# Last stage: rows of two tables fetched by one gather of 8 KB rows, or by two of 4 KB rows with rings of their own

## What is computed

```python
def _peer(h, wq, keys, u, v):              # h: tokens x 1024; u, v: 16384 x 1024
    q = (xt @ wq).reshape(P_BLOCK, P_HEADS, 2, P_HALF)
    s = jnp.einsum('nhpd,hpkd->nhpk', q, keys)
    ...
    top_s, pos = lax.top_k(cand_s, P_TOPK) # 16 picks for each of 8 heads
    idx = jnp.take_along_axis(cand_i, pos, axis=-1).reshape(P_BLOCK, P_HEADS * P_TOPK)
    g = jax.nn.softmax(...)
    act = jax.nn.gelu(jnp.einsum('nd,ned->ne', xt, u[idx]), approximate=False)
    return jnp.einsum('ne,ned->nd', g * act, v[idx])
```

## Time and profile before

| | us |
|---|---|
| median of 3 runs | 4033.4 |
| lowest, highest | 4031.19, 4033.41 |
| the profiled execution, its own time | 4033.23 |
| span of the profile, first to last instruction | 4031.5 |
| last stage: first gather issued to last gather issued | 2664.6 to 3996.7 |

### The profile page before, as it was taken

The page is one execution under the profiler, slowest core; times in us unless marked ns, Lnnn a source line. Parts: engine busy times, 40 slices in busy tenths (PEclk is TensorE's granted clock), DMA queues, the critical chain, the costliest instruction groups (busy, mean ns, idle before and its releaser), DMA issues. The chain is left out here.

```text
span 4031.5 us, 37513 instructions
## 1 busy us (share of the span) xinstructions
PE 3402.5 (84%) x11902; PEld 1525.5 (38%) x11903; DVE 1934.3 (48%) x3945; ACT 677.6 (17%) x1600; POOL 928.9 (23%) x811
## 2 busy tenths in 40 slices
PE   7988999668899978999868967689878888788877
PEld 3345444422333322333325445444333333333332
DVE  5834222522223323233325235476666766676676
ACT  1011211000000000000002125312222222222221
POOL 2000000021222222021221031014444444444443
PEclk9999999789999998999989988899999899999988
DMA  9825423369998999297975100239999999999997
GB/s 328 284 108 177 167 101 133 125 242 386 375 386 343 387 386 367 71 386 278 383 305 195 53 7 1 76 133 409 422 421 413 421 404 414 421 405 421 412 421 317
DMA packets 194149, 1157.36 MB, mean 287 GB/s; under 512 B 25659, under 2 KB 27995, under 8 KB 74356
## 3 DMA queue, kind: packets, MB, share of 16 engines
q1 hardware_dynamic: 97140, 565.17, 36.1%
q0 software_dynamic: 80576, 564.05, 34.2%
q10 hardware_dynamic: 16320, 26.75, 2.2%
HBM read 1128.96 MB, written 48.68 MB: 292 GB/s over the span
## 5 line engine op out<-in xcount | busy, mean ns | idle before, releaser
L2558 DVE SCALAR_TENSOR_TENSOR mod<-q_uv,mix 128x1024 f32<-128x1024 f32 x512 | 627.4, 1225 | 389.9 <-DMA q_uv<-in_peer_uv,q_picks 384.6
L1149 PE MATMUL ps<-wt,e_xT 128*64 128x512 f32 x3200 | 733.4, 613 | 94.4 <-DMA wt<-in_w_exp 93.6
L2263 POOL DMA_INDIRECT q_uv<-in_peer_uv,q_picks x512 | 571.2, 1116 | 996.6 <-PE ps L2355 719.1
L2355 PE MATMUL ps<-q_uv,q_dg 128*128 128x512 f32 x1024 | 491.6, 634 | 118.5 <-ACT q_dg L2432 118.3
L2355 PE MATMUL ps<-q_uv,tri 128*128 128x512 f32 x1024 | 494.3, 639 | 104.6 <-ACT tri L2432 104.6
L1129 POOL COPY wt<-e_land 128x2048 f32<-128x2048 f32 x124 | 237.1, 1912 | 1020.8 <-DMA e_land<-in_w_exp 1020.8
L1149 PEld LDWEIGHTS ps<-wt,e_xT 128*64 128x64 f32 x3200 | 238.3, 141 | 579.8 <-issue 433.2
L1149 PE MATMUL ps<-wt,e_aT 128*64 128x512 f32 x1600 | 357.4, 599 | 21.6 <-ACT e_aT L1202 21.6
L2355 PEld LDWEIGHTS ps<-q_uv,q_dg 128*128 128x128 f32 x1024 | 202.7, 203 | 398.6 <-issue 398.6
L2355 PEld LDWEIGHTS ps<-q_uv,tri 128*128 128x128 f32 x1024 | 205.6, 205 | 390.2 <-issue 390.2
L454 PE MATMUL ps<-hT,wt 128*128 128x512 f32 x640 | 285.0, 601 | 1.5 <-DVE wt L781 1.5
(11 more groups left out here) (446 smaller groups left out, 3329.8 us busy)
## 6 DMA issues: line engine op xcount, KB each, us to landing
wt<-in_w_exp SPq DMA_DIRECT2D x260, 1024.0 KB, 17.5
e_land<-in_w_exp SPq DMA_DIRECT2D x124, 1024.0 KB, 24.6
wt<-in_w_in_units SPq DMA_DIRECT2D x15, 2048.0 KB, 10.4
mod<-in_w_mod_units SPq DMA_DIRECT2D x48, 512.0 KB, 5.6
scratch_xs<-const_zeros SPq DMA_DIRECT2D x8, 2080.0 KB
mod<-in_w_ada_units SPq DMA_DIRECT2D x32, 512.0 KB, 6.5
p_ring<-in_w_in SPq DMA_DIRECT2D x7, 2048.0 KB, 10.4
e_xg<-scratch_xs ACTq DMA_DIRECT2D x104, 128.0 KB
```

The source lines that it names most:

```text
L1149: ins = nc.tensor.matmul(ps[64 * h:64 * h + 64, at, :], lhs[:, k % 4, 64 * (k // 4):64 * (k // 4) + 64], wt[:, u, a, h * W:(h + 1) * W], s ...
L2263: pool.indirect_dma_start(out=uv[:, n % NR, :, :].rearrange("p a d -> p (a d)"), out_offset=None, in_=A["peer_uv"], in_offset=bass.Indirec ...
L2355: last = nc.tensor.matmul(acc(t)[:, c, :], dg(n), uv[:, n % NR, 1, c * W:(c + 1) * W], start=fresh, stop=closing)
L2558: dve.scalar_tensor_tensor(junk[:, n % 2, :], uv[:, n % NR, 0, :], 1.0, mix[:, tile_of(k), :], ALU.mult, ALU.mult, accum_out=ap[:, k % 2, ...
```

## The change

Each step now fetches the row of `u` and the row of `v` by a transfer each, from two tables, 128 rows of 4 KB (512 KB) each. The memory of the ring is the same, now seen as 20 halves (`rows`): `NU` = 8 of them are a ring for `u`, given back by VectorE's dot (`s_u`), and `NV` = 12 are a ring for `v`, given back by TensorE (`s_v`). VectorE waits for the transfer of `u` alone, TensorE for that of `v` alone. GpSimd issues `u` of step `n`, then `v` of step `n`. The two waits at the start of the stage are moved to the first `v` slots that lie on the keys and the projection.

```diff
         uv = sb("uv", [P, NR, 2, D])
+        NU, NV = 8, 2 * NR - 8
+        rows = uv[:, :, :, :].rearrange("p n a d -> p (n a) d")
...
-        s_uv = [sem(f"uv{i}") for i in range(NR)]
+        s_gu = [sem(f"gu{i}") for i in range(NU)]
+        s_gv = [sem(f"gv{i}") for i in range(NV)]
...
                 for n in range(TOTAL):
                     if n % BATCH == 0:
                         pool.wait_ge(s_r, n // BATCH + 1)
-                    if n == KEYS:
+                    if n >= NU:
+                        pool.wait_ge(s_u, n - NU + 1)
+                    pool.indirect_dma_start(out=rows[:, n % NU, :], out_offset=None, in_=A["peer_u_2"],
+                                            in_offset=bass.IndirectOffsetOnAxis(ap=picks[:, n:n + 1], axis=0)
+                                            ).then_inc(s_gu[n % NU], 16)
+                    if n == 2 * KEYS - NU:
                         pool.wait_ge(s_kt, 1)
-                    if n == WOUT:
+                    if n == 2 * WOUT - NU:
                         pool.wait_ge(s_full, 2 * NT)
-                    if n >= NR:
-                        pool.wait_ge(s_v, n - NR + 1)
-                    pool.indirect_dma_start(out=uv[:, n % NR, :, :].rearrange("p a d -> p (a d)"), out_offset=None,
-                                            in_=A["peer_uv"],
+                    if n >= NV:
+                        pool.wait_ge(s_v, n - NV + 1)
+                    pool.indirect_dma_start(out=rows[:, NU + n % NV, :], out_offset=None, in_=A["peer_v_2"],
                                             in_offset=bass.IndirectOffsetOnAxis(ap=picks[:, n:n + 1], axis=0)
-                                            ).then_inc(s_uv[n % NR], 16)
+                                            ).then_inc(s_gv[n % NV], 16)
...
-                    pe.wait_ge(s_uv[n % NR], 16 * (n // NR + 1))
+                    pe.wait_ge(s_gv[n % NV], 16 * (n // NV + 1))
...
-                        last = nc.tensor.matmul(acc(t)[:, c, :], dg(n), uv[:, n % NR, 1, c * W:(c + 1) * W],
+                        last = nc.tensor.matmul(acc(t)[:, c, :], dg(n), rows[:, NU + n % NV, c * W:(c + 1) * W],
...
-                    dve.wait_ge(s_uv[n % NR], 16 * (n // NR + 1))
+                    dve.wait_ge(s_gu[n % NU], 16 * (n // NU + 1))
...
-                    dve.scalar_tensor_tensor(junk[:, n % 2, :], uv[:, n % NR, 0, :], 1.0, mix[:, tile_of(k), :],
+                    dve.scalar_tensor_tensor(junk[:, n % 2, :], rows[:, n % NU, :], 1.0, mix[:, tile_of(k), :],
```

More of the change, by code:

```diff
@@ L2681 @@
 SCRATCH = dict(xs=[(NBLK + 2) * BLK, D], modr=[24, W], o=[3, T, OW], line=[3, AH, LINE], lines=[P, 3, AH, LINE])
-FLAT = {"x": (T, D), "ctx_2": (TC, D), "peer_uv": (NK * NK, 2 * D)}
+FLAT = {"x": (T, D), "ctx_2": (TC, D), "peer_u_2": (NK * NK, D), "peer_v_2": (NK * NK, D)}
 def kernel(**inputs):
@@ L2690 @@
     arrays, A, K = {}, {}, {}
-    inputs["peer_uv"] = np.concatenate([np.asarray(inputs.pop("peer_u_2")), np.asarray(inputs.pop("peer_v_2"))], -1)
     gate, up, down = (np.asarray(inputs.pop(n)).reshape(NE, 4, 2, P, D) for n in ("w_gate", "w_up", "w_down"))
```

## The result

The changed kernel takes 4191.5 us (median of 4 runs, 4183.97 to 4197.31), the kernel before 4032.3 beside it: 1.0389 times as long, 95% interval 1.0376 to 1.0402. That is 159 us slower, where +147 were forecast. The profiled execution took 4196.48 us, its span 4194.7.

What follows compares the result with a forecast made beforehand. The DMA engines were taken as full before, GpSimd as the bound after: 2.49 + 0.36 = 2.85 us against 2.55 over 489 steps is +147 us, start and end 0, giving 4180 us from 4033.2; range 4050 to 4300.

Steps and rivals of the forecast that it cites:

- most marks: Signs expected in the changed profile: 1024 gathers, mean above 1.0, GpSimd busy about 1100 us, 360 to 380 GB/s, no dips.
- Twice the issues, 1.245 us by gather and not by byte: GpSimd in the last stage: a gather's price ignores its bytes, so two per step take 2.49 us.
- Smaller rows, 2.55 us a step: DMA engines in the last stage: 4 KB rows take 2.49 to 2.61 us a step, the middle 2.55.
- Held gathers, the mechanism: A GpSimd gather starting inside VectorE's two-input dot waits until the dot ends, then needs its last 0.81 us.
- Held gathers, the factor 0.6 x 0.60 = 0.36 us a step: GpSimd's held time per step: chance value 0.60 us scaled by today's 0.6, giving 0.36, between 0 and 0.60.
- But VectorE's dot 8 steps back is then long over: GpSimd's wait ahead of each `u` gather: it holds the queue, but the dot it needs is already done.
- More slots, 0 at the start and at most 12 us in the dips: Rings: running further ahead regains at most 12 us of rate dips at TensorE's queries; start at most 5 us, taken as 0.
- Waits that split, no cost: TensorE waiting for `v` alone: no cost; without cover by three steps' matmuls, at most 1.25 us per group of four.
- Slots do not help: Ring in the last stage: extra slots cannot offset the 2.85 us step, because the ring is empty and not full.
- Rival B: DMA engines stay the bound, GpSimd just keeps up: step 2.54 to 2.65 us, 4028 to 4082 us; chance 0.14.
- Rival D: Each dot catches a gather at its beginning: step from 3.15 us, bound 3.71, 4327 to 4600 us; chance 0.07.

Runs made afterwards that it cites:

- experiment 5: The changed kernel run again as it is, beside others on one chip: 4183.7 us, 1.0378.
- Experiment 11: The changed kernel with GpSimd waiting once for two `u` halves at even steps and once for two `v` halves at odd ones: 4055.8 us, 1.0069.
- Experiment 4: The changed kernel with a dot that reads one SBUF operand, a constant replacing the token's values: 4054.0 us, 1.0054.
- experiments 3: The changed kernel with rows of 2 KB instead of 4 KB, columns 512 to 1023 left out: 4222.5 us, 1.0472.
- experiment 7: The kernel before with two gathers of 2 KB rows per step in its old ring, given back by TensorE: 4229.1 us, 1.0496.
- 9: Two 4 KB gathers per step in the old ring, plus an already met wait for VectorE's dot ahead of the `u` gather: 4204.9 us, 1.0425.
- 10: Two 4 KB gathers per step in the old ring, plus the met wait for TensorE repeated between them: 4198.3 us, 1.0420.
- experiment 8: The kernel before with a head's query matmuls spread over eight steps instead of two: 4029.9 us, 0.9997.
- 6: The changed kernel with rings of 10 and 10 halves in place of 8 and 12: 4187.1 us, 1.0390.
- 1: The kernel before with two gathers of 4 KB rows per step in its old ring, given back by TensorE, one wait a step: 4062.7 us, 1.0074.
- Experiments 2: The kernel before with an extra gather of 8 bytes a partition each step, with its own ring and wait: 4070.6 us, 1.0095.
- 12: The kernel before, one 8 KB gather a step, with one more already met wait on GpSimd: 4028.8 us, 0.9998.

## Why the prediction came out right, and where its reasons did not hold

The sign was right, and so was the size (4180 for 4191.5), but the size by luck. In the changed kernel's own profile most marks are there: 1024 gathers with mean 1036 and 1134 ns, GpSimd busy 530.6 + 580.8 = 1111 us, 366 GB/s, VectorE waiting 400.8 us, no dip at 3220 us. One mark can't be read: too many records are missing there for a time to landing. The experiments show that this sum stands on a wrong split. Over before, 4055.8 - 4029.7 = 26 us belong to the two gathers of 4 KB. The other 4191.5 - 4055.8 = 136 us come with the second wait per step, which the prediction priced at nothing. (The two sum to 162, not 159, because the kernel before took 4032.3 beside the one and 4029.7 beside the other. From the repeat in experiment 5, 4183.7 us, it is 128.)

- *Twice the issues, 1.245 us by gather and not by byte:* right. The gaps are 0.30 us in each kernel, and a gather that nothing holds takes some 0.94 us with 8 bytes, 2 KB, 4 KB and 8 KB a partition.
- *Smaller rows, 2.55 us a step:* right. Experiment 11 moves 409 GB/s in the undisturbed stretch, 2.56 us, and 405 in the steady one, 2.59 us.
- *Held gathers, the mechanism:* right. Experiment 4 takes the second operand away and the held time with it.
- *Held gathers, the factor 0.6 x 0.60 = 0.36 us a step:* wrong in what it stands for, and named as the weakest term. The changed kernel has 0.29. Experiment 11, the same work without the late counts, has 1024 x (1.001 - 0.941) = 61 us, 0.12 a step. The scaling took gathers and dots as half random. They are locked: the held time is what is left between 2.49 us and the pace that the landings allow. With DMA engines that are full it is small. With landings that come early (experiments 3 and 7) each `v` gather is caught and the step is 2.97 us. In the changed kernel the late counts empty the queue again and again, and in the 10 to 20 us after each the rate is near 320 GB/s. There the gathers are held: from 3115 to 3127 us one takes 1.20 us in the mean and from 3175 to 3195 us 1.14, but 0.96 from 3130 to 3165 us, at 410 GB/s. So 0.12 becomes 0.29.
- *"But VectorE's dot 8 steps back is then long over":* the dot is, and the wait was priced at 0 for that. This is the step that failed. A second wait on GpSimd in each step, even one that is already met (9, 10), brings late counts, 0.13 us of plain waiting a step and more held time. The sum was right because one term was too large by about what the missing one cost.
- *More slots, 0 at the start and at most 12 us in the dips:* the start gained a little, 303 GB/s over the first 86 us where the earlier trace rows have 272, which is 86 x 31 / 421 = 6 us. The dips are worth nothing measurable in experiment 8.
- *Waits that split, no cost:* right. In experiment 11 TensorE's waits at L2362 are put down to ScalarE's diagonals (169.0 and 72.9 us) and none to a `v` gather.
- *"Slots do not help":* true for their number (6). How they are waited for is worth 136 us (11).
- *Rival B* (the DMA engines stay the bound, 4028 to 4082) is what the change would have been with one wait a step: 4055.8 us, held time 0.12 us under its limit of 0.16. *Rival D*, the rhythm in which each dot catches a gather, exists too, in a milder form than its 3.15 us and more: 2.97 us in experiments 3 and 7, though not with 4 KB rows.

What stays open is why counts arrive late. Shown is that it goes with the waits per step on GpSimd: one more brings it (1 to 9 and 10), half of them takes it away (changed kernel to 11). Two waits alone are not enough. Experiments 2, 3 and 4 have two waits and two gathers a step and no late counts, and 12 has two waits and one gather. In those either the DMA engines are not full (3), or the dots hold nothing (4), or the second gather is tiny (2). So it needs full DMA engines, held gathers of rows and the second wait together, as far as these kernels go. How these delay a count of VectorE to VectorE itself is not shown. Two causes do not fit. The loading of instructions moves 60 packets from 2664 us on, as in experiment 11, and none of them between 3248 and 3292 us, around the stop shown above. And TensorE's clock (mean granted clock 0.89 in the steady stretch, 0.94 before) does not enter a count that VectorE raises for itself; TensorE is busy for 1082 of 1410 us.

Nor is it shown whether the recording has a part in it: every run here was recorded, and the kernels with late counts are those whose records have the large holes. The two also go together in time. In the 20 us before each of the 28 waits at L2271 over 0.33 us from 2750 us on, the changed kernel's trace has 2.7 semaphore records per us in the mean, and in the 10 us after it 7.5, where experiments 1 and 11 have 14.4 and 14.5 in the median of their slices of 10 us. The Trainium skill (NOTIFIC — the notification-queue block, "7.1 Overflow: three behaviours, one of which stalls the engine") says that a full record queue, by its setting, discards the new record, overwrites the oldest, or stalls the producer of the records. The first two would give the holes and the third the stops; no run here shows which setting held, or tests it.

## What to carry to other kernels

Count the gathers and the waits on GpSimd, not the bytes: an indirect gather of 128 rows cost its 1.25 us here whether a row had 8 bytes or 8 KB, so one gather of a joined row is better than two of half rows (0.7% here at best). Where two are needed, wait once for several slots; two conditions were worth 128 to 136 us here. And a prediction whose total comes true is not yet explained: look at short slices before trusting a mean, since 365 GB/s was 410 with holes.

## What the runs showed of the hardware that was not expected

- Counts can arrive late on every engine at once. VectorE went on 3.5 and 4.5 us after it had raised its own count, and a gather of GpSimd started over 14 us after TensorE had raised the count that it needed. In ordinary times GpSimd's next gather starts 0.27 us after TensorE's step ends.
- In the same kernels many semaphore records are missing from the trace (25800 to 27000 over the whole span in the changed kernel and experiments 5, 6, 9 and 10, against 37600 in experiments 1 to 4 and 11). The profile then names releasers from stages long over ("yT", "remote"). Such a name is a sign to look for missing records. It is no proof of late counts: experiment 7 has 36100 records and none of its parts of `choose` starts late.
- A lock between two engines can make less work slower: in the old ring rows of 2 KB take 4229.1 us, rows of 4 KB 4062.7.
- The gathers of 4 KB rows keep the DMA engines at 405 to 409 GB/s (experiment 11, steady and undisturbed stretch), those of 8 KB at 417 to 421, both at a share of 1.01 to 1.03.
